# A gating layernorm moved from feature-major to token-major form, and three weight buffers moved in SBUF

## The reference, cut to what matters

```python
def _layernorm(x, g, b):
    mu = jnp.mean(x32, axis=-1, keepdims=True)
    var = jnp.mean(jnp.square(x32 - mu), axis=-1, keepdims=True)
    return ((x32 - mu) * lax.rsqrt(var + EPS)).astype(x.dtype) * g + b

def _spatial_gating(u, v, ln_g, ln_b, w_s, b_s):
    u = jax.nn.gelu(u)
    v = _layernorm(jax.nn.gelu(v), ln_g, ln_b)
    bn, ln, ch = v.shape
    vr = v.reshape(bn, ln // SG_CHUNK, SG_CHUNK, SG_GROUPS, ch // SG_GROUPS)
    mixed = jnp.einsum("gpq,bnqgc->bnpgc", w_s, vr) + b_s.T[None, None, :, :, None]
    return u * mixed.reshape(bn, ln, ch)
```

## Time and profile before

| | |
|---|---|
| runs before, us | 2766.63, 2755.2, 2766.84 |
| profiled execution, its own time, us | 2758.92 |
| its span, us | 2757.0 |
| mean granted TensorE clock | 0.964 of full speed |
| busy: PE, PEld, DVE, ACT, POOL, us | 2546.5, 2044.8, 1498.7, 728.1, 1047.7 |

### The profile page before, as it was taken

How to read it: one execution, slowest core, us unless ns; L and a number is a source line. 1 busy time by engine, 2 the same in 40 slices (tenths; PEclk the granted TensorE clock), 3 DMA queues, 4 the chain that set the end, 5 groups by cost and what they waited for, 6 DMA issues and landing times.

```text
span 2757.0 us, 33015 instructions
## 1 busy us (share of the span) xinstructions
PE 2546.5 (92%) x12016; PEld 2044.8 (74%) x12016; DVE 1498.7 (54%) x2191; ACT 728.1 (26%) x1208; POOL 1047.7 (38%) x493
## 2 busy tenths in 40 slices
PE   8999999999989879999996999979899999999997
PEld 4888777777767757877674777868577777777775
DVE  4795155757501166545697644466764444444446
ACT  4411334344300155122321444432220000000112
POOL 2344333333257423447641011113553333334444
PEclk9999999999999889999998799989999999999999
DMA  8575444444365942333311231341211111111111
GB/s 345 186 260 216 157 143 138 136 134 148 118 237 196 350 165 99 99 121 119 132 39 44 69 98 58 100 152 47 69 61 46 46 46 46 46 46 46 46 46 69
DMA packets 131232, 325.24 MB, mean 118 GB/s; under 512 B 11568, under 2 KB 59248, under 8 KB 125616
## 3 DMA queue, kind: packets, MB, share of 16 engines
q1 hardware_dynamic: 91232, 215.63, 23.7%
q10 hardware_dynamic: 39888, 108.08, 10.9%
HBM read 248.57 MB, written 70.39 MB: 116 GB/s over the span
## 4 chain that ended last, share of the span: by engine, by line
PE 50%; DVE 8%; issue 3%; ACT 1%; DMA 0%; DVEq 0%; SPq 0%; ACTq 0%
PE pb L478 36%; PE g L2980 6%; PE g L3053 2%; PE pb L2980 1%; PE g L3033 1%; DVE zcs L2245 1%; PE g L2961 1%; DVE f_spare L2454 1%; PE g L2834 1%; DMA kept_in<-cs_d 0%; DVE xl L2157 0%; PE g L2959 0%; DVE hl L2524 0%; DVE x L2596 0%; DVE ml L2461 0%
## 5 line engine op out<-in xcount | busy, mean ns | idle before, releaser
L841 POOL TENSOR_TENSOR w_hi<-w_raw,one 128x1024 fp32r<-128x1024 f32 x191 | 394.8, 2067 | 1531.9 <-PE pb L478 1135.3
L844 POOL TENSOR_TENSOR w_lo<-w_raw,w_hi 128x1024 fp32r<-128x1024 f32 x191 | 511.3, 2677 | 15.0
L478 PE MATMUL pb<-xh,w_hi 128*128 128x512 f32 (+1 forms) x1224 | 482.5, 394 | 25.7 <-POOL w_lo L844 11.8
L478 PE MATMUL pb<-xh,w_lo 128*128 128x512 f32 (+1 forms) x1224 | 474.0, 387 | 0.0
L478 PE MATMUL pb<-xl,w_hi 128*128 128x512 f32 (+1 forms) x1224 | 473.9, 387 | 0.0
L478 PE MATMUL pb<-mh,w_hi 128*128 128x512 f32 x704 | 282.0, 400 | 14.9 <-DVE ml L2461 7.3
L478 PEld LDWEIGHTS pb<-xh,w_hi 128*128 128x128 f32 x1224 | 233.5, 191 | 81.4 <-POOL w_lo L844 13.6
L478 PE MATMUL pb<-mh,w_lo 128*128 128x512 f32 x704 | 279.9, 398 | 0.0
L478 PE MATMUL pb<-ml,w_hi 128*128 128x512 f32 x704 | 279.8, 397 | 0.0
L478 PEld LDWEIGHTS pb<-xl,w_hi 128*128 128x128 f32 x1224 | 232.8, 190 | 51.0
L478 PEld LDWEIGHTS pb<-xh,w_lo 128*128 128x128 f32 x1224 | 233.8, 191 | 49.6 <-issue 1.0
(11 more groups left out here) (408 smaller groups left out, 4617.9 us busy)
## 6 DMA issues: line engine op xcount, KB each, us to landing
w_raw<-in_wall SPq DMA_DIRECT2D x190, 512.0 KB, 3.6
mod_later<-in_modw SPq DMA_DIRECT2D x28, 1024.0 KB, 6.5
proj_d<-stage ACTq DMA_DIRECT2D x40, 512.0 KB, 2.7
at_bias<-in_bias SPq DMA_DIRECT2D x64, 192.0 KB, 2.6
mod_raw<-in_modt SPq DMA_DIRECT2D x8, 1024.0 KB, 11.2
w_raw<-in_wall ACTq DMA_DIRECT2D x15, 512.0 KB, 7.3
svt<-vt_d ACTq DMA_DIRECT2D x12, 512.0 KB, 4.6
vc<-proj_d SPq DMA_DIRECT2D x10, 512.0 KB, 5.6
```

Source lines behind the costliest of these rows:

```text
L478: mm = pe.matmul(pb[bank][:, 0:n], w[:, b, wc:wc + P], x[:, k, tokens], start=(count == 0), stop=(count == total - 1))
L841: nc.gpsimd.tensor_tensor(w_hi[:, b, :], w_raw[:, b, :], one[:, 0:1].to_broadcast([P, 1024]), ALU.mult).then_inc(w_high, 1)
L844: nc.gpsimd.tensor_tensor(w_lo[:, b, :], w_raw[:, b, :], w_hi[:, b, :], ALU.subtract).then_inc(w_split, 1)
```

## The change: what it does

The statistics of the gating norm are taken after the transposition, with tokens on the partitions, so that a mean is a sum along the free axis of one partition.

- PE no longer runs the eight products of the two `gating_means`. The 16 transposes stand ahead of the key tile and act on `gelu(v)` itself. Before them stand four small products (64 stationary columns, 128 moving) of the 1/256 matrix with `sgw_sb`, which give the row sums of `w_s`. PE waits for the load of `sgw_sb` there.
- ACT copies the transposed blocks to `vtok` in eight instructions of 128x256, each with a sum per partition. It then squares them with the negated mean as bias in eight more, again with a sum, takes a root of 128x8, and applies reciprocal root and shifted mean in eight of 128x256. The waits that stand ahead of the first key read-out are now for PE's transposes.
- DVE no longer subtracts, inverts and multiplies whole tiles. It has a few instructions of 128x2 and 128x8 on a new buffer `vstat`, and two of 128x128 that add the offset times the row sums to `sgb_sb`. The final bias addition becomes a multiply by the gain and an addition.
- SP waits for one count of ACT in place of two counts of PE and DVE before the first `bias_load`.
- `w_raw`, `w_hi` and `w_lo` are allocated after the small constants instead of before them, and `vstat` (128 bytes per partition) is added ahead of them; all that lies above begins 128 bytes higher.

```diff
--- before.py
+++ after.py
@@ -125,9 +125,6 @@
             return t
 
 
-        w_raw = keep("w_raw", [P, 2, 1024])
-        w_hi = keep("w_hi", [P, 2, 1024], F32R)
-        w_lo = keep("w_lo", [P, 2, 1024], F32R)
         col = keep("col", [P, NCOL])
         modx = keep("modx", [P, 72])
         modc = keep("modc", [P, 72])
@@ -144,6 +141,10 @@
         both_gain = keep("both_gain", [P, KT])
         both_root = keep("both_root", [P, KT])
         dec = keep("dec", [P, NC, 8])
+        vstat = keep("vstat", [P, 4, NCX])
+        w_raw = keep("w_raw", [P, 2, 1024])
+        w_hi = keep("w_hi", [P, 2, 1024], F32R)
+        w_lo = keep("w_lo", [P, 2, 1024], F32R)
         ident, mean_d, mean_v, mean_g = (mat[:, n, :] for n in range(4))
         arena = place["next"]
 
@@ -368,8 +369,7 @@
         low_keys, z_at = at("zkr", [P, TA], arena + 107 * KB, F32R)
         zcs, a = at("zcs", [P, 8, T], z_at)
         hpad, a = at("hpad", [P, 2, T + TAPS - 1], a)
-        vsq, b = at("vsq", [P, 2, T], a)
-        vroot, _ = at("vroot", [P, T], a)
+        vsq, b = at("vsq", [P, NCX, C], a)
         vtok, c_ = at("vtok", [P, NCX, 256], b)
         sgw_sb, c_ = at("sgw_sb", [P, 4, P], c_)
         sgb_sb, _ = at("sgb_sb", [P, 2, P], c_)
@@ -783,8 +783,7 @@
                 bc, br, j = step_of(s)
                 sp.dma_start(at_bias[:, s % 4, :], bias6[br, bc, s // 16, j]).then_inc(bias_in[s % 4], 16)
 
-            sp.wait_ge(y_pe, 2)
-            sp.wait_ge(y_dve, 3)
+            sp.wait_ge(y_act, 2)
             for s in range(4):
                 bias_load(s)
             for s in range(STEPS):
@@ -1449,27 +1448,32 @@
                 return pb[u % 2]
 
             u_k, u_v, u_q, u_k1, _ = PAIR_UNITS
+            act.wait_ge(y_pe, 2)
+            for n in range(NCX):
+                v = act.activation(vtok[:, n, :], g[:, n // 2, C * (n % 2):C * (n % 2) + C], ACT.Copy,
+                                   accum_out=vstat[:, 0, n:n + 1])
+            v.then_inc(y_act, 1)
             pair_k_high(0, 0, pair_unit(u_k))
             act.wait_ge(y_dve, 1)
-            act.activation(vsq[:, :, :], zcs[:, 6:8, :], ACT.Square).then_inc(y_act, 1)
+            act.wait_ge(xl_ready, 6 * KT)
+            for n in range(NCX):
+                v = act.activation(vsq[:, n, :], vtok[:, n, :], ACT.Square, bias=vstat[:, 0, n:n + 1],
+                                   accum_out=vstat[:, 1, n:n + 1])
+            v.then_inc(y_act, 1)
+            act.wait_ge(y_act, 2)
+            act.activation(vstat[:, 1, :], vstat[:, 1, :], ACT.Sqrt, scale=1.0 / C,
+                           bias=epsc[:, 0:1]).then_inc(y_act, 1)
             for n in (1, 2):
                 pair_k_high(0, n, pair_unit(u_k + n))
-            act.wait_ge(y_pe, 2)
-            act.activation(vroot[:, :].rearrange("p (u n) -> p u n", u=2), g[:, 4:6, :], ACT.Sqrt,
-                           bias=epsc[:, 0:1]).then_inc(y_act, 1)
             pair_values(0, 0, pair_unit(u_v), bank_free[u_v % 2])
             keys_across(0)
             pair_values(0, 1, pair_unit(u_v + 1), bank_free[(u_v + 1) % 2])
             act.wait_ge(y_dve, 3)
-            for t in range(2):
-                n, m = COL["sg_g"] + t, COL["sg_b"] + t
-                v = act.activation(zcs[:, 6 + t, :], zcs[:, 6 + t, :], ACT.Identity,
-                                   scale=col[:, n:n + 1], bias=col[:, m:m + 1])
+            for n in range(NCX):
+                v = act.activation(vtok[:, n, :], vtok[:, n, :], ACT.Identity, scale=vstat[:, 1, n:n + 1],
+                                   bias=vstat[:, 2, n:n + 1])
             v.then_inc(y_act, 1)
             pair_values(0, 2, pair_unit(u_v + 2), bank_free[u_v % 2])
-            act.wait_ge(y_pe, 3)
-            act.activation(vtok[:, :, :].rearrange("p (a n) c -> p a (n c)", a=4), g[:, 0:4, :],
-                           ACT.Copy).then_inc(y_act, 1)
             for n in range(2):
                 pair_q_high(0, n, pair_unit(u_q + n))
             queries_across(0)
@@ -1477,7 +1481,7 @@
             act.activation(zcs[:, 2:4, :], zcs[:, 0:2, :], ACT.Square).then_inc(z_act, 1)
             for n in range(2):
                 if n == 0:
-                    act.wait_ge(y_pe, 4)
+                    act.wait_ge(y_pe, 3)
                 pair_k_high(1, n, pair_unit(u_k1 + n))
             act.wait_ge(y_dve, 5)
             act.dma_start(cs_d[0:2].rearrange("t p n -> p t n"), zcs[:, 6:8, :]).then_inc(kept_out, 16)
@@ -2252,21 +2256,21 @@
             for k in range(KT):
                 ctx_low(k)
             taps(5, 14)
+            nc.vector.tensor_scalar(vstat[:, 3, 0:2], col[:, COL["sg_b"]:COL["sg_b"] + 2], float(C), None, ALU.mult)
+            dve.wait_ge(y_act, 1)
+            nc.vector.tensor_scalar(vstat[:, 0, :], vstat[:, 0, :], -1.0 / C, None, ALU.mult).then_inc(y_dve, 1)
+            dve.wait_ge(y_dve, 1)
             dve.wait_ge(y_pe, 1)
             for t in range(2):
-                v = nc.vector.tensor_tensor(zcs[:, 6 + t, :].rearrange("p (u n) -> p u n", u=2),
-                                            zcs[:, 6 + t, :].rearrange("p (u n) -> p u n", u=2),
-                                            g[:, 4:6, :], ALU.subtract)
-            v.then_inc(y_dve, 1)
+                nc.vector.scalar_tensor_tensor(sgb_sb[:, t, :], g[:, 4, P * t:P * t + P], vstat[:, 3, t:t + 1],
+                                               sgb_sb[:, t, :], ALU.mult, ALU.add)
             for n, (first, last) in enumerate(((14, 17), (17, 18), (18, 20))):
                 pair_k_low(0, n, pb[(u_k + n) % 2], bank_free[(u_k + n) % 2])
                 taps(first, last)
-            dve.wait_ge(y_act, 2)
-            nc.vector.reciprocal(vroot[:, :], vroot[:, :]).then_inc(y_dve, 1)
+            dve.wait_ge(y_act, 3)
+            nc.vector.reciprocal(vstat[:, 1, :], vstat[:, 1, :]).then_inc(y_dve, 1)
             dve.wait_ge(y_dve, 2)
-            nc.vector.tensor_tensor(zcs[:, 6:8, :], zcs[:, 6:8, :],
-                                    vroot[:, :].unsqueeze(1).to_broadcast([P, 2, T]), ALU.mult)\
-              .then_inc(y_dve, 1)
+            nc.vector.tensor_tensor(vstat[:, 2, :], vstat[:, 0, :], vstat[:, 1, :], ALU.mult).then_inc(y_dve, 1)
             for n, (first, last) in enumerate(((20, 23), (23, 25))):
                 taps(first, last)
                 pair_q_low(0, n, pb[(u_q + n) % 2], bank_free[(u_q + n) % 2])
@@ -2292,13 +2296,13 @@
                                       [:, :, first:first + 32]).then_inc(at_sp, 1)
 
             at_stage(0)
-            dve.wait_ge(y_pe, 4)
-            dve.wait_ge(sg_in, 32)
+            dve.wait_ge(y_pe, 3)
             for t in range(2):
-                v = nc.vector.tensor_tensor(
+                n = COL["sg_g"] + t
+                v = nc.vector.scalar_tensor_tensor(
                     zcs[:, 6 + t, :].rearrange("p (n q) -> p n q", q=CH),
-                    g[:, 2 * t:2 * t + 2, :].rearrange("p a (n q) -> p (a n) q", q=CH),
-                    sgb_sb[:, t, :].unsqueeze(1).to_broadcast([P, NCX, CH]), ALU.add)
+                    g[:, 2 * t:2 * t + 2, :].rearrange("p a (n q) -> p (a n) q", q=CH), col[:, n:n + 1],
+                    sgb_sb[:, t, :].unsqueeze(1).to_broadcast([P, NCX, CH]), ALU.mult, ALU.add)
             v.then_inc(y_dve, 1)
             dve.wait_ge(y_dve, 4)
             nc.vector.tensor_tensor(zcs[:, 6:8, :], zcs[:, 6:8, :], zcs[:, 4:6, :], ALU.mult)\
@@ -2882,37 +2886,31 @@
                                        stop=True)
                 mm.then_inc(z_pe, 1)
 
-            def gating_means(src):
-                for n in range(2):
-                    for t in range(2):
-                        mm = pe.matmul(g[:, 4 + n, :], mean_v, src[:, t, H * n:H * n + H], start=(t == 0),
-                                       stop=(t == 1))
-                mm.then_inc(y_pe, 1)
-
             evicted(pe, UNIT[T_PAIR])
-            gating_means(zcs[:, 6:8, :])
-            pe.wait_ge(xl_ready, 6 * KT)
-            pe.wait_ge(xh_ready, 6 * KT)
-            pe_tile(pe, T_PAIR)
-            pe.wait_ge(y_act, 1)
-            pe.wait_ge(y_dve, 1)
-            gating_means(vsq[:, :, :])
-            pe_tile(pe, T_PAIR + 1)
-            pe.wait_ge(y_act, 3)
+            pe.wait_ge(sg_in, 32)
+            for q in range(4):
+                t, r = q // 2, 64 * (q % 2)
+                mm = pe.matmul(g[r:r + 64, 4, P * t:P * t + P], mean_v[:, 0:64], sgw_sb[:, q, :], start=True,
+                               stop=True)
+            mm.then_inc(y_pe, 1)
             for n in range(NCX):
                 for t in range(2):
                     o = (2 * n + t) * P
                     mm = pe.transpose(g[:, o // H, o % H:o % H + P], zcs[:, 6 + t, CH * n:CH * n + CH], ident)
             mm.then_inc(y_pe, 1)
+            pe.wait_ge(xl_ready, 6 * KT)
+            pe.wait_ge(xh_ready, 6 * KT)
+            pe_tile(pe, T_PAIR)
+            pe_tile(pe, T_PAIR + 1)
             pe_tile(pe, T_PAIR + 2)
```

(4 more changed lines are left out.)

## The result

The changed kernel takes 2724.3 us (median of four runs, 2718.2 to 2732.2) against 2764.5 us for the kernel before on the same chip: a ratio of 0.9866, with a 95% interval of 0.9834 to 0.9898. The forecast was 2752 us, its range 2743 to 2762. Experiments found the reason: the step that was costed at nothing, the moved buffers, is worth about 1%.

A forecast was written before the change was run, and what follows sets the result against it. TensorE was taken to bound the kernel, with DVE setting the changed stretch's end. The profiled 2758.92 us less 9.6 gave 2749.3, the three-run median 2757.0; the forecast was 2752 us, range 2743 to 2762.

The forecast's parts named there:

- the moved buffers: Buffers at new addresses, over the whole kernel: taken as 0, with ends of a gain and a loss of 1 ns per matmul.
- the rival: Over the whole kernel, new addresses make each matmul dearer: 12 us at 1 ns; 2776 at 2 ns; chance 0.08.
- The last sign of being wrong: Over the weight products: the prediction is wrong if their mean moves by a nanosecond or more.
- The norm's sum: In the stretch up to the first low query, the new norm gains 9.6 us, the forecast gain; chance 0.42.
- Value tile unmoved: Start of PE's value tile: 1445.47 us as before, since the 1.2 us DVE saves are eaten behind POOL's w_lo.
- the lighter work: DVE from 1432.57 us to the first low key: 1.05 us instead of 2.26, so 1.2 us less.
- The clock: PE at the value tile, after 5.9 us of idleness: a start at the lower clock costs 1.65 us, bounds 0 and 1.65.
- The query: End of the stretch: the first low query starts at 1467.6 instead of 1477.20 us, 9.6 us earlier, by PE's chain.
- DVE behind POOL: DVE's six taps ahead of the low query: POOL's split adds 1.7 and 2.25 us, so they end at 1468.0.
- ACT's covers: ACT finishes before it is needed: 4.3 us ahead at the second high key, 3.8 at the third value read-out.
- PE's wait at the next means: PE's wait at conv_means for DVE's last tap stays near 17 us but ends near 1490.
- POOL gets in early: POOL's split enters before 1432.57 us, DVE loses 3.9 us, value tile 2.3 late; gain 7.3 us, 2754.6; chance 0.30.

The follow-up runs named there:

- the places alone: The kernel before with its old norm, but every buffer at the address it has after the change; 2728.8 us, ratio 0.9897.
- the norm alone: The new norm with all old buffers at their old addresses and vstat in a free place; 2745.2 us, ratio 0.9947 to the kernel before.
- The kernel that keeps PE busy there: The changed kernel with POOL's fourth pair tile split held until the last tap, second low key after 4 taps instead of 6; 2728.9 us, 0.987.

## Why the prediction was wrong

**The step that failed** is the sentence on the moved buffers: "the rows give no price: I take 0, with ends of a gain and a loss of 1 ns per matmul". What the runs show in its place is 6.3 to 6.6 ns less per weight product of 512 columns at the full clock, and 2728.8 instead of 2759.0 us from the addresses alone. No row of before held that price. But the step set its ends by hand, at 0.25% of a 394 ns mean, and the gain end never came into the range: its floor of 2743 us is 14.3 us of the norm and 5 us of scatter. And the mean of 394 ns was the wrong yardstick. It is a duration that overlaps the next; the interval between starts (233.5 ns) is what is paid. The sign that the rival gave ("slower") was wrong too: it treated the old places as the cheap ones, where their distance was one of the dear ones. The last sign of being wrong (the mean of the weight products moves by a nanosecond or more) did come, 394 to 393 ns, but a sixth of the size of the interval's move.

**How much of the faster products reaches the end** depends on what ends last, and here the views differ by stage. The windows of the kernel before (window, its us, then busy us and count of PE, PEld, DVE, ACT, POOL, the granted clock, DMA's share, GB/s) in an attention stage and in the feed-forward stage:

```profile
480.00:740.00 260.00, 241.09 (x1309) 203.08 (x1308) 173.82 (x332) 104.80 (x187) 82.66 (x32) 1.00 0.41 134
1920.00:2700.00 780.00, 752.74 (x3177) 597.61 (x3176) 398.52 (x385) 99.04 (x123) 335.64 (x147) 0.99 0.16 50
```

The same windows of the places alone:

```profile
480.00:740.00 260.00, 239.92 (x1260) 205.65 (x1259) 168.25 (x318) 100.43 (x176) 88.55 (x32) 0.95 0.39 126
1920.00:2700.00 780.00, 750.09 (x3234) 609.43 (x3233) 406.31 (x394) 103.10 (x129) 338.90 (x151) 0.99 0.15 48
```

In the feed-forward stage 3234 products pass in the window instead of 3177 at the same clock: from DVE's first pass over `cb` to the end it takes 736.7 instead of 752.2 us. About 3,200 products at 6.3 ns would be 20 us; 15.5 arrived. In the attention stage the window holds fewer products, 1260 against 1309, at a granted clock of 0.95 against 1.00, and by the starts of the same products the kernel is 8.4 us ahead at 483 us and only 0.9 us at 760 us. The gain there was given back by the clock. That isn't chance: the window has a clock of 1.00 in all four traces with an interval of 233.4 ns or more, 0.98 at a distance of 128 over, and 0.94 or 0.95 in the other twelve. So the clock, too, goes with the distance, which fits the times between the ends of the table; what in the faster stream lowers it isn't shown. In the whole kernel 7,400 intervals at 6.3 ns would be 47 us, and 30 arrived. The same program scatters as well: in two executions of the kernel after the window from 1500 to 1920 us has a clock of 0.95 and 0.92, and what follows the copy that opens the next stage differs by 8.5 us.

```profile
1500.00:1920.00 420.00, 386.75 (x2213) 320.00 (x2212) 231.56 (x650) 172.26 (x418) 80.24 (x37) 0.95 0.28 89
```

```profile
1500.00:1920.00 420.00, 390.69 (x2178) 324.38 (x2176) 226.54 (x645) 169.20 (x414) 74.78 (x34) 0.92 0.27 87
```

**The norm's sum came out, two of its terms did not.** To keep the places out of it, the norm alone (its first tap is 3.64 us earlier than in the kernel before):

```profile
1428.93 1.86 DVE L2259 TENSOR_SCALAR vstat<-col 128x2 f32<-128x2 f32 x1
...
1431.43 0.67 DVE L2220 SCALAR_TENSOR_TENSOR zkr<-pb,ka 64x512 fp32r<-64x512 f32 x1
...
1441.83 0.77 PE L478 MATMUL pb<-xh,w_hi 128*128 128x512 f32 x1 [4.42 <-DVE zkr L2220]
...
1453.23 8.90 DVE L2249 SCALAR_TENSOR_TENSOR zcs<-hpad,col,zcs 128x1024 f32<-128x1024 f32 x6 [0.16 <-issue]
1464.31 0.68 DVE L2230 TENSOR_TENSOR ql<-pb,qa 64x512 fp32r<-64x512 f32 x1 [2.18 <-ACT qa L1385]
```

- *Value tile unmoved.* From the first tap it starts after 62.84 us, to the hundredth as before (1445.47 less 1382.63). The time was right and the way there was not: the lighter work never came. The 128x2 instruction was priced at 0.21 us and took 1.86, up to the end of POOL's `w_hi`, so DVE needed 2.50 us to the first low key (1428.93 to 1431.43) instead of the forecast 1.05, and 2.26 before. In return POOL's `w_lo` cost the six taps less (7.42 us, before 7.65).
- *The clock.* PE idles ahead of the value tile for 4.42 us instead of 1.15, and its first product takes 0.77 us instead of the 0.47 of the earlier trace rows: the lower clock. From there to the first value read-out (1449.77) it takes 7.94 us instead of 5.88, so the clock cost 2.06 us, where 1.65 was charged. The kernel that keeps PE busy there shows the 0.47 again.
- *The query.* 9.25 us earlier (forecast 9.6). PE and ACT come last by 2.18 us here. In the kernel after, with faster products, DVE comes last and the gap is gone.
- *DVE behind POOL.* Here the forecast 1.7 + 2.25 = 3.95 us did not come: the six taps took 8.90 us and lost 1.7, for POOL's split began only at 1458.46 and its `w_lo` in the sixth tap instruction (1461.13). So DVE was ready 2.2 us before PE, and the two did not "nearly meet". The loss of 3.9 us (11.05 less 7.2) is seen in the kernel after, where PE's query tile, and with it the split, begins earlier.
- *ACT's covers* held. The first, for one: in the kernel after the second high key was done at 1433.8 us and DVE wanted it at 1436.3, 2.5 us of cover (4.3 forecast).
- *PE's wait at the next means* stays, 18.3 us after and 17.3 with the norm alone against 17.3 in the earlier trace rows:

```profile
PE g L2885 <- DVE zcs L2249: 18.3, 1, 18.3
```

One more small miss: PE idles 4.72 us ahead of the third key unit with the norm alone and 5.31 us in the kernel after, against 3.34 in the earlier trace rows, since the transposes take less than the mean records did and, in the kernel after, the products before it are faster.

**The rival "POOL gets in early" did not happen**: `w_hi` lasted 13.73 us after and 13.43 us with the norm alone, against 12.26 in the earlier trace rows. The Trainium skill, "SBUF — State Buffer", section "Who interferes with whom", has the lock held for one instruction. Three long splits, past which eight to ten taps went each time, speak against a fair turn after every instruction; the short ones (2.11 and 2.37 us), after which DVE pays, agree with it. The same section says that only the pair of ports shared by DVE and GpSimd causes contention. No run here can say whether that is all: PE has a price here, 233 or 227 ns, that depends on where its two operands stand, and whether this is a collision of reads isn't shown.

**Still open.** What happens in a product with a dear distance isn't shown, only that the distance decides. Remainders other than 0, 32, 64, 128 and 192 weren't tried. What decides whether POOL gets in or waits isn't known. And the norm alone gained 14.6 us in time by its ratio, against 9.7 us that its marks show in and right behind the stretch; its execution was 3.6 us ahead at the first tap already, where nothing differs, and the interval (5.5 us either way) covers the rest.

## What to carry to other kernels

Before tuning the order of a kernel bound by TensorE, measure the interval between its products from start to start, work out the distance in bytes between the stationary and the moving operand's buffers, and try the padding that makes it a multiple of 256: here 64 bytes were worth 30 us of 2759. A small new buffer in the arena shifts everything behind it, so an edit that moves addresses has a price of its own, of either sign, on every product; split it off and run it alone. And a cost that no row shows gets ends as wide as its count allows: thousands of products turn 6 ns into a result.

## What the runs showed of the hardware

- Weight products (128x128 by 512 columns, fp32r) at the full clock follow each other after 226.9 to 227.1 ns when the distance of their operands in a partition is a multiple of 256 bytes (24576, 29184, 29440), 229.1 ns at 64 over, and 232.4 to 233.5 ns at 32, 128 and 192 over.
- Moving both operands by 32 bytes together changes nothing (32.70 us for 144 products either way).
- Faster products don't always shorten a stage: in the attention stage (480 to 740 us) the granted clock was 0.95 instead of 1.00 with them, and they brought nothing.
- A POOL instruction of 1.9 us lasted 13.7 us beside taps that DVE ran back to back, and in other places 2.1 us, where DVE then lost 1.7 us and more.
